# A second layer's attention on one core: values of two units in one product, reciprocals folded into the turn

## The chip, the cores and the metric

One core of one Trainium2 chip. The metric is the device time of one launch in microseconds, the median of the runs shown. Engines: PE is TensorE, DVE VectorE, ACT ScalarE, POOL GpSimd, SP SyncE.

## What is computed

Two transformer layers in fp32 over 256 tokens of width 1024. The change lies in the second one's windowed attention: 16 query heads of 64 columns, 4 key heads, 16 meta tokens that every query sees, and a sink logit for each head. Cut to that:

```python
s_band = jnp.einsum('bqhgd,bkhd->bhgqk', qi, kb).astype(jnp.float32) * scale
s_band = jnp.where(mask, s_band, NEG_INF_2)
s_meta = jnp.einsum('bqhgd,bmhd->bhgqm', qi, k_meta).astype(jnp.float32) * scale
s_sink = jnp.broadcast_to(sink_g[None, :, :, None, None], s_meta.shape[:-1] + (1,))
p = jax.nn.softmax(jnp.concatenate([s_band, s_meta, s_sink], axis=-1), axis=-1)
...
return (jnp.einsum('bhgqk,bkhd->bqhgd', p_band, vb)
        + jnp.einsum('bhgqm,bmhd->bqhgd', p_meta, v_meta))
```

The other half of this layer's attention is differential: 8 heads, two softmaxes each, their difference times the values.

## The kernel before

All weights come as a stream of blobs of 128 x 2048 fp32 (`raw`), which ScalarE copies to a rounded high part (`hi`, L891) and VectorE subtracts to a low part (`lo`, L1901). A product of the weights is then three fp32r products (high by high, high by low, low by high; `product`, L530 to L532, or wider forms at L709 and L711). Every engine has its whole order written out by hand and they meet through semaphores.

In the second layer PE goes through blobs `m2 = 0..33` in two parts each. After each part comes `slot(q)` with `q = 2 * m2 + part`. Small work of the attention is done in the slots, one **unit** a slot, in a pipeline several slots deep. A unit is two heads (`u = 0, 1`) for 128 queries; two neighbouring units `U = 2c, 2c + 1` are the same heads for the first and second 128 queries (`unit_place`). Units 0 to 15 (`U < S_UNITS`) are the windowed attention and units 16 to 31 the differential one; `U0` is 22. Unit U runs so, its slot counted as `q - U0 - U`:

- 0, PE: scores of both heads, four products of 272 columns in fp32r (L1802), to banks 4 and 5.
- 1, DVE: `unit_front` scales, masks and takes the maximum (L2103), into `sc`. ACT: exp of both heads with their sums (L1204) and of the sink (L1207). DVE: `unit_back` adds the sink and takes the reciprocal (L2119, L2120). ACT: `sc` times the reciprocal, one ACTIVATE for each head (L1239), which signals `u_norm`.
- 2, PE: `unit_turn` turns 2 x 2 tiles of 128 x 128 (L1736) and one tile of 48 columns with both heads' meta probabilities (L1739) by `pe.transpose` against `ident`. DVE copies the four tiles to `puT` (L2449), ACT the fifth to `pmT` (L1215).
- 3, PE: `unit_values`: meta (L1750) and two key tiles (L1755) for each head, into 64 columns of the array each, 128 moving columns, plain fp32. ACT and DVE take high and low parts of the result (L1223, L2455).

In one slot of PE, `unit_turn` of a unit stands ahead of `unit_values` of the unit before it, and the scores of a later unit come last. So slot 24 (U0 + 2) has a turn and no values, slots 25 to 39 have both, and slot 40 has values of unit 15 behind the turn of unit 16. A differential unit turns two tiles and a tile of 32 columns; its difference of softmaxes is made before the turn by DVE, and its values are products of full width (L1758, L1760).

`PE` in the text is the group of matmul records, `PEld` that of weight loads. The trace gives one record for a transpose and two for a plain fp32 product.

Of the kernel before, what the change touches and what calls it, by code (L numbers as in the profile page):

```python
# [44 lines left out]
SECOND = TOK + QUAD  # L45
XSTEP = 320


# [139 lines left out]
def build(nc, w, x, meta, consts, turns, rows, grow, out):  # L188

    with ExitStack() as ctx:  # L190
        def sem(name):
            return ctx.enter_context(nc.semaphore(name))
# [119 lines left out]
        rrow2 = at("rrow2", [P, TOK], F32, top[0])  # L312
        ql = [new("ql0", [P, 2, TOK], F32R)]
        assert top[0] <= 3 * BLOB
# [6 lines left out]
        vb_meta = new("vb_meta", [P, D])  # L321
        top[0] += 1536 - 960
        dT_h = at("dT_h", [P, KC, TOK], F32R, top[0])
# [7 lines left out]
        sc = [new("sc0", [P, SECOND + KEYS]), new("sc1", [P, SECOND + KEYS])]  # L331
        puT = new("puT", [P, 4, P])
        pmT = new("pmT", [P, P])
        scratch2 = new("scratch2", [P, 2 * DH])
# [121 lines left out]
        u_pr = sem("u_pr")  # L456
        u_norm = sem("u_norm")
        u_pt = sem("u_pt")
# [424 lines left out]
        def _(act):  # L883
# [300 lines left out]
            for q in range(2 * OUT2):  # L1184
# [9 lines left out]
                if q in VALUES_AT:  # L1194
                    values_out(VALUES_AT[q])
                if q == 14:
                    act.wait_ge(lam_s, 1)
                    act.activation(lam[:, 2:4], lam[:, 0:2], ACT.Exp).then_inc(lam_e, 1)
# [11 lines left out]
                if 0 <= U < UNITS:  # L1210
                    act.wait_ge(u_pt, U + 1)
                    if U:
                        act.wait_ge(u_o, U)
                    rows_used = QUAD + N_META if U < S_UNITS else QUAD
                    act.activation(pmT[0:rows_used, :], ps[0:rows_used, 7, 32:32 + P], ACT.Copy).then_inc(u_ptm, 1)  # L1215
                U = q - U0 - 3
                if 0 <= U < S_UNITS:
                    act.wait_ge(u_o, U + 1)
                    if U == 0:
                        act.wait_ge(kd_out[0], 16 * 5)  # L1220
                        act.wait_ge(kd_out[1], 16 * 2)
                    cc, t = unit_place(U)
                    act.activation(sT_h[:, cc, t * P:(t + 1) * P], ps[:, 7, 288:288 + P],  # L1223
                                   ACT.Copy).then_inc(d_hi, 1)
                elif S_UNITS <= U < UNITS:
                    act.wait_ge(u_o, U + 1)
                    act.wait_ge(u_pr, U + 1)
                    if U >= S_UNITS + 3:

                        act.wait_ge(d_ps, U - S_UNITS - 2)  # L1230
                    first = usoft[:, U % 4, 5, 0:1]
                    act.activation(o_junk[:], ps[:, 7, 288:288 + P], ACT.Square, scale=first,
                                   accum_out=ostat[:, U % 3, 0:1])
                    act.activation(o_tok[U % 3][:], ps[:, 7, 288:288 + P], ACT.Copy, scale=first).then_inc(d_o, 1)
                U = q - U0 - 1
                if 0 <= U < S_UNITS:
                    act.wait_ge(u_pr, U + 1)
                    for u in range(2):
                        ins = act.activation(scores(U, u), scores(U, u), ACT.Copy, scale=usoft[:, U % 4, 5, u:u + 1])  # L1239
                    ins.then_inc(u_norm, 1)  # L1240
                U = q - U0 - 5
# [7 lines left out]
                if q % 2 == 1 and m - 2 in KEY_BLOBS:  # L1249
                    keys_high(m - 2)  # L1250
                if q % 2 == 1 and m - 2 in QUERIES:
                    queries_high(m - 2)
# [176 lines left out]
        def _(pe):  # L1429
# [296 lines left out]
            def unit_turn(U):  # L1726

                pe.wait_ge(u_norm if U < S_UNITS else u_pr, U + 1)
                if U:
                    pe.wait_ge(u_ptd, U)  # L1730
                    pe.wait_ge(u_ptm, U)
                result_read(U - 1)
                heads = 2 if U < S_UNITS else 1
                for u in range(heads):
                    for kt in range(NT):
                        pe.transpose(ps[:, 6, (2 * u + kt) * P:(2 * u + kt + 1) * P],  # L1736
                                     scores_of_tile(U, u, kt), ident)
                both = SECOND + N_META if heads == 2 else SECOND
                pe.transpose(ps[0:both - TOK, 7, 32:32 + P], sc[U % 2][:, TOK:both], ident).then_inc(u_pt, 1)  # L1739

            def unit_values(U):

                pe.wait_ge(u_ptd, U + 1)
                pe.wait_ge(u_ptm, U + 1)
                result_read(U)
                (cc, t), o = unit_place(U), ps[:, 7, 288:288 + P]
                if U < S_UNITS:
                    for u in range(2):
                        a = (2 * (cc // 4) + u) * DH
                        pe.matmul(ps[u * DH:(u + 1) * DH, 7, 288:288 + P], vs_meta[:, a:a + DH], pmT[:],  # L1750
                                  start=True, stop=False)
                    for kt in range(NT):
                        for u in range(2):
                            a = (2 * (cc // 4) + u) * DH
                            m = pe.matmul(ps[u * DH:(u + 1) * DH, 7, 288:288 + P], vs[:, kt, a:a + DH],  # L1755
                                          puT[:, 2 * u + kt, :], start=False, stop=kt == 1)
                else:
                    pe.matmul(o, pmT[:], vb_meta[:, cc * P:(cc + 1) * P], start=True, stop=False)  # L1758
                    for kt in range(NT):
                        m = pe.matmul(o, puT[:, kt, :], vb[:, kt, cc * P:(cc + 1) * P], start=False, stop=kt == 1)  # L1760
                m.then_inc(u_o, 1)

            def slot(q):
# [15 lines left out]
                if 0 <= U + 1 < UNITS:  # L1779
                    unit_turn(U + 1)  # L1780
                if 0 <= U < S_UNITS:
                    unit_values(U)
                U = q - U0 - 5
# [6 lines left out]
                if 0 <= U < UNITS:  # L1790
                    cc, t = unit_place(U)
                    if t == 0:
                        pe.wait_ge(q_in[query_of(U)], 32)
                        pe.wait_ge(kb_in[key_slot(U)], keys_loaded(U))
                    if U:
                        pe.wait_ge(u_max, U)
                    if U > 5:
                        pe.wait_ge(d_lo, U - 5)
                    qT, kT = qs if U < S_UNITS else qd, kB[key_slot(U)]
                    for u in range(2):  # L1800
                        for v in range(2):
                            m = pe.matmul(ps[:, 4 + u, 0:KEYS], qT[u][:, cc, t * P:(t + 1) * P],  # L1802
                                          kT[:, 2 * u + v, 0:KEYS].bitcast(F32R), start=v == 0, stop=v == 1)
                    m.then_inc(u_sc, 1)
# [83 lines left out]
        def _(dve):  # L1888
# [225 lines left out]
            def unit_back(U):  # L2114
# [3 lines left out]
                if U < S_UNITS:  # L2118
                    link(dve, "dve", dve.tensor_tensor(st[:, 4, :], st[:, 4, :], st[:, 3, :], ALU.add))  # L2119
                ins = dve.reciprocal(st[:, 5, :], st[:, 4, :])  # L2120
                if U >= S_UNITS:
                    link(dve, "dve", ins)
                    link(dve, "dve", dve.scalar_tensor_tensor(out=st[:, 3, 0:1], in0=st[:, 5, 1:2], scalar=neglam[:],
                                                              in1=st[:, 4, 0:1], op0=ALU.mult, op1=ALU.mult))
                    first, second = scores(U, 0), scores(U, 1)
                    ins = dve.scalar_tensor_tensor(out=first, in0=second, scalar=st[:, 3, 0:1],
                                                   in1=first, op0=ALU.mult, op1=ALU.add)
                ins.then_inc(u_pr, 1)

# [270 lines left out]
            for q in range(2 * OUT2):  # L2400
# [42 lines left out]
                U = q - U0 - 2  # L2443
                if 0 <= U < UNITS:
                    dve.wait_ge(u_pt, U + 1)
                    if U:
                        dve.wait_ge(u_o, U)
                    n = 4 if U < S_UNITS else 2
                    dve.tensor_copy(puT[:, 0:n, :], ps[:, 6, 0:n * P].rearrange("p (a q) -> p a q", a=n)).then_inc(  # L2449
                        u_ptd, 1)  # L2450
                U = q - U0 - 3
                if 0 <= U < S_UNITS:
                    dve.wait_ge(d_hi, U + 1)
                    cc, t = unit_place(U)
                    dve.tensor_tensor(sT_l[:, cc, t * P:(t + 1) * P], ps[:, 7, 288:288 + P],  # L2455
                                      sT_h[:, cc, t * P:(t + 1) * P], ALU.subtract).then_inc(d_lo, 1)
                if q in (50, 54):
# [296 lines left out]
```

## Time and profile before

| | |
|---|---|
| median of the 3 runs | 869.05 us (868.91 to 869.34) |
| the profiled execution | 870.0 us, of which its span is 868.2 |
| PE busy | 858.9 us, 99% of the span |
| DVE busy | 626.8 us, 72% |
| ACT busy | 478.7 us, 55% |
| windowed units, first turn to last values | 473.3 to 553.0 us (record starts) |

A row of a group reads: line, engine, operation, output <- inputs, shape, xcount, then busy time and the mean of one in ns, then the idle time ahead of it. A matmul's mean is the time of one record from its start to its end, 270 ns and more, and successive ones overlap. What it costs PE is the distance from its start to the next start, which the timeline gives; a line of the timeline merges records of one kind ("x4").

### The profile page before, as it was taken

To read this page: it belongs to the slowest core of one execution; us is meant where nothing else is said; L and a number is where in the kernel's file an instruction comes from. 1 tells how busy PE (TensorE), PEld (TensorE's weight loads), DVE (VectorE), ACT (ScalarE), POOL (GpSimd) and SP (SyncE) were. 2 spreads that over 40 slices of the span, in tenths; PEclk is the share of its full clock that TensorE was granted. 3 is DMA by queue.
4 is the path that set the end of the run, shared out by engine and by line. 5 is a ranking of instruction groups with operands and counts; after the bars stand their busy time and mean duration, and the time that the engine had idled before them with its cause. 6 is when DMAs were issued, how large, how long until landed. Compare 5 with 4: busy or idle time off the path is not lost.

```text
span 868.2 us, 13077 instructions
## 1 busy us (share of the span) xinstructions
PE 858.9 (99%) x4812; PEld 736.2 (85%) x4812; DVE 626.8 (72%) x985; ACT 478.7 (55%) x769; POOL 68.9 (8%) x96
## 2 busy tenths in 40 slices
PE   8999999999999999999999999999999999999997
PEld 6887788888888888889999888888888888888885
DVE  6867677666876666677688887887766876666665
ACT  6546633434644444446687887676653654444443
POOL 1000000000200000002122010132300100000000
PEclk9999999999999999999999999999999999999999
DMA  8955344554565555452766535745475365455531
GB/s 322 415 213 193 110 168 160 183 182 169 186 242 194 193 193 189 143 177 72 249 229 235 173 107 184 259 170 195 152 285 170 122 237 186 172 200 186 178 145 48
DMA packets 30334, 164.70 MB, mean 190 GB/s; under 512 B 3840, under 2 KB 5632, under 8 KB 12880
## 3 DMA queue, kind: packets, MB, share of 16 engines
q1 hardware_dynamic: 27840, 157.71, 51.1%
q10 hardware_dynamic: 2448, 6.37, 2.2%
q8 instruction: 29, 0.48, 0.2%
q14 instruction: 17, 0.14, 0.0%
HBM read 157.02 MB, written 3.83 MB: 185 GB/s over the span
## 4 chain that ended last, share of the span: by engine, by line
PE 97%; DVE 1%; DMA 1%; ACT 0%; issue 0%; SPq 0%; DVEq 0%; POOL 0%; ACTq 0%
PE ps L530 18%; PE ps L532 18%; PE ps L531 18%; PE ps L696 8%; PE ps L681 8%; PE ps L700 4%; PE ps L677 4%; PE ps L709 3%; PE ps L1802 2%; PE ps L711 2%; PE ps L565 1%; PE ps L1736 1%; PE ps L1760 1%; PE ps L1755 1%; PE ps L1750 1%; DMA raw<-weights 1%
## 5 line engine op out<-in xcount | busy, mean ns | idle before, releaser
L1901 DVE TENSOR_TENSOR wlo<-raw,whi 128x2048 fp32r<-128x2048 f32 x134 | 306.9, 2292 | 148.6 <-ACT whi L891 148.0
L891 ACT ACTIVATE whi<-raw 128x2048 fp32r<-128x2048 f32 x134 | 256.3, 1913 | 177.9 <-PE ps L532 108.5
L530 PE MATMUL ps<-whi,xT 128*128 128x512 f32 x192 | 76.8, 400 | 0.0
L532 PE MATMUL ps<-whi,xT 128*128 128x512 f32 x192 | 75.0, 391 | 0.0
L531 PE MATMUL ps<-wlo,xT 128*128 128x512 f32 x192 | 74.9, 390 | 0.0
L1371 POOL TENSOR_TENSOR stat<-stat,cst 128x1 f32<-128x1 f32 x10 | 11.9, 1201 | 489.2 <-DVE stat L1921 260.8
L530 PE MATMUL ps<-whi,fT_h 128*128 128x512 f32 x128 | 50.2, 392 | 0.0
L532 PE MATMUL ps<-whi,fT_l 128*128 128x512 f32 x128 | 49.8, 389 | 0.0
L531 PE MATMUL ps<-wlo,fT_h 128*128 128x512 f32 x128 | 49.8, 389 | 0.0
L530 PE MATMUL ps<-x_all,whi 128*128 128x272 f32 x160 | 46.4, 290 | 0.0
L532 PE MATMUL ps<-x_all,wlo 128*128 128x272 f32 x160 | 46.2, 289 | 0.0
L531 PE MATMUL ps<-x_all,whi 128*128 128x272 f32 x160 | 46.2, 288 | 0.0
L1204 ACT ACTIVATE sc<-sc,usoft 128x272 f32<-128x272 f32 x64 | 32.6, 511 | 19.1 <-DVE usoft L2112 16.0
L532 PEld LDWEIGHTS ps<-whi,xT 128*128 128x128 f32 x192 | 36.0, 188 | 7.8
L530 PEld LDWEIGHTS ps<-whi,xT 128*128 128x128 f32 x192 | 36.1, 188 | 7.4
L531 PEld LDWEIGHTS ps<-wlo,xT 128*128 128x128 f32 x192 | 36.1, 188 | 7.0
L681 PE MATMUL ps<-x_all,whi 128*128 128x512 f32 x176 | 42.0, 391 | 0.0
L530 PE MATMUL ps<-whi,x_all 128*128 128x512 f32 x96 | 38.0, 396 | 0.0
L696 PE MATMUL ps<-x_all,whi 128*128 128x512 f32 x160 | 38.0, 390 | 0.0
L532 PE MATMUL ps<-whi,x_all 128*128 128x512 f32 x96 | 37.8, 393 | 0.0
L681 PEld LDWEIGHTS ps<-x_all,whi 128*128 128x128 f32 x176 | 32.3, 188 | 6.3
L531 PE MATMUL ps<-wlo,x_all 128*128 128x512 f32 x96 | 37.5, 391 | 0.0
(351 smaller groups left out, 1885.3 us busy)
## 6 DMA issues: line engine op xcount, KB each, us to landing
raw<-weights SPq DMA_DIRECT2D x134, 1024.0 KB, 4.8
kB<-key_parts SPq DMA_DIRECT2D x20, 272.0 KB, 3.3
key_parts<-knat SPq DMA_DIRECT2D x4, 544.0 KB, 3.0
cst<-consts SPq DMA_DIRECT2D x1, 1371.0 KB, 13.4
kswap<-kraw SPq DMA_DIRECT2D x8, 136.0 KB, 2.4
raw<-weights SPq DMA_DIRECT2D x4, 256.0 KB, 6.1
raw<-weights SPq DMA_DIRECT2D x2, 512.0 KB, 7.5
gate_a<-gain_rows ACTq DMA_DIRECT2D x2, 512.0 KB, 8.1
```

The costliest lines, as they stand in the source:

```text
L530: pe.matmul(o, lh, rh, start=first, stop=False)
L531: pe.matmul(o, lh, rl, start=False, stop=False)
L532: return pe.matmul(o, ll, rh, start=False, stop=last)
L677: pe.matmul(ps[:, bank0 + j, 0:TOK], vl[:, k, j * P:(j + 1) * P], x[:, 0, k, :], start=k == 0, stop=False, skip_group_check=True)
L681: m = pe.matmul(ps[:, bank0 + j, :], vh[:, k, j * P:(j + 1) * P], x[:, :, k, :], start=False, stop=k == KC - 1, skip_group_check=True)
L696: pe.matmul(ps[:, bank0 + j, :], vh[:, k, j * P:(j + 1) * P], x[:, :, k, :], start=k == 0, stop=False)
L700: m = pe.matmul(ps[:, bank0 + j, 0:TOK], vl[:, k, j * P:(j + 1) * P], x[:, 0, k, :], start=False, stop=k == KC - 1)
L709: pe.matmul(ps[:, bank + j, :], vh[:, k, j * P:(j + 1) * P], x2[:, :, k, :], start=k == 0, stop=False)
L711: m = pe.matmul(ps[:, bank + j, 0:TOK], vl[:, k, j * P:(j + 1) * P], x2[:, 0, k, :], start=False, stop=k == KC - 1)
L891: act.activation(whi[s][:], raw[s][:], ACT.Copy).then_inc(split_hi, 1)
L1204: ins = act.activation(scores(U, u), scores(U, u), ACT.Exp, bias=st[:, 2, u:u + 1], accum_out=st[:, 4, u:u + 1])
L1901: dve.tensor_tensor(wlo[s][:], raw[s][:], whi[s][:], ALU.subtract).then_inc(split_lo, 1)
```

## The change

For the windowed units alone:

- The ACTIVATEs that multiply by the reciprocals are gone. VectorE makes two diagonal matrices `unit_diag` (`ident` times the reciprocal, one for each head) in `unit_back`, and the turn is a plain fp32 product of the probabilities with that diagonal instead of a transpose. The tile with the meta probabilities becomes two products, of 32 and 16 columns, as each head has its own diagonal.
- The copy of the four turned tiles goes from VectorE to ScalarE. `puT` and `pmT` are doubled, with one half for each unit of a pair.
- The values are made once for a pair of units (`pair_values`), with 256 moving columns instead of 128, in every second slot. The high and low parts are taken once a pair.
- `queries_high` of blobs 9 and 12 goes one slot later, behind `values_out`. PE's scores wait for fewer semaphores. `ql0`, `puT` and what lies around them have other addresses.

```diff
@@ ScalarE
                 if q in VALUES_AT:
                     values_out(VALUES_AT[q])
+                    if m - 3 in QUERIES:
+                        queries_high(m - 3)
...
                     act.wait_ge(u_pt, U + 1)
-                    if U:
-                        act.wait_ge(u_o, U)
+                    if U > 1:
+                        act.wait_ge(u_o, U - U % 2 if U < S_UNITS else U - 1)
...
-                    act.activation(pmT[0:rows_used, :], ps[0:rows_used, 7, 32:32 + P], ACT.Copy).then_inc(u_ptm, 1)
-                U = q - U0 - 3
-                if 0 <= U < S_UNITS:
-                    act.wait_ge(u_o, U + 1)
+                    if U < S_UNITS:
+                        act.activation(puT[:, :, U % 2, :], ps[:, 6, :].rearrange("p (a q) -> p a q", a=4),
+                                       ACT.Copy).then_inc(u_ptd, 1)
+                    act.activation(pmT[0:rows_used, U % 2, :], ps[0:rows_used, 7, 32:32 + P], ACT.Copy).then_inc(u_ptm, 1)
+                U = q - U0 - 4
+                if 0 <= U < S_UNITS and U % 2 == 0:
+                    act.wait_ge(u_o, U + 2)
...
+                    act.activation(sT_h[:, cc, :], ps[:, 7, PAIR:PAIR + TOK], ACT.Copy).then_inc(d_hi, 2)
...
-                U = q - U0 - 1
-                if 0 <= U < S_UNITS:
-                    act.wait_ge(u_pr, U + 1)
-                    for u in range(2):
-                        ins = act.activation(scores(U, u), scores(U, u), ACT.Copy, scale=usoft[:, U % 4, 5, u:u + 1])
-                    ins.then_inc(u_norm, 1)
@@ TensorE
             def unit_turn(U):
...
+                for u in range(2):
+                    for kt in range(NT):
+                        pe.matmul(ps[:, 6, (2 * u + kt) * P:(2 * u + kt + 1) * P], scores_of_tile(U, u, kt),
+                                  unit_diag[:, U % 2, u, :], start=True, stop=True)
+                for u, (a, b) in enumerate(((TOK, SECOND), (SECOND, SECOND + N_META))):
+                    m = pe.matmul(ps[a - TOK:b - TOK, 7, 32:32 + P], sc[U % 2][:, a:b], unit_diag[:, U % 2, u, :],
+                                  start=True, stop=True)
+                m.then_inc(u_pt, 1)
+
+            def pair_values(U):
+
+                pe.wait_ge(u_ptd, U + 2)
+                pe.wait_ge(u_ptm, U + 2)
+                result_read(U)
+                cc, _ = unit_place(U)
+                for u in range(2):
+                    a = (2 * (cc // 4) + u) * DH
+                    pe.matmul(ps[u * DH:(u + 1) * DH, 7, PAIR:PAIR + TOK], vs_meta[:, a:a + DH],
+                              pmT[:].rearrange("p a q -> p (a q)"), start=True, stop=False)
+                for kt in range(NT):
+                    for u in range(2):
+                        a = (2 * (cc // 4) + u) * DH
+                        m = pe.matmul(ps[u * DH:(u + 1) * DH, 7, PAIR:PAIR + TOK], vs[:, kt, a:a + DH],
+                                      puT[:, 2 * u + kt].rearrange("p a q -> p (a q)"), start=False, stop=kt == 1)
+                m.then_inc(u_o, 2)
...
-                if 0 <= U < S_UNITS:
-                    unit_values(U)
+                if 1 <= U < S_UNITS and U % 2 == 1:
+                    pair_values(U - 1)
@@ VectorE
                 if U < S_UNITS:
                     link(dve, "dve", dve.tensor_tensor(st[:, 4, :], st[:, 4, :], st[:, 3, :], ALU.add))
+                    link(dve, "dve", dve.reciprocal(st[:, 5, :], st[:, 4, :]))
+                    if U >= 2:
+                        dve.wait_ge(u_pt, U - 1)
+                    for u in range(2):
+                        ins = dve.tensor_scalar(unit_diag[:, U % 2, u, :], c("ident"), st[:, 5, u:u + 1], None, ALU.mult)
+                    ins.then_inc(u_diag, 1)
```

How the order moves is seen at two places. The first is PE, two successive slots with the turns of units 3 and 4 (`sc` is the probabilities, `x_all` the tokens' products between the slots, left out here). Before, both slots read alike but for the buffer; the first one:

```order
L1736 MATMUL ps<-cst,sc_143 128x128 [waits u_ptm,d_lo,u_ptd,u_norm]
L1736 MATMUL ps<-cst,sc_143 128x128 x3
L1739 MATMUL ps<-cst,sc_143 48x128
L1750 MATMUL ps<-pmT,vs_meta 64x128 [waits d_lo,u_ptm,u_ptd]
L1750 MATMUL ps<-pmT,vs_meta 64x128
L1755 MATMUL ps<-puT,vs 64x128 x4
L1802 MATMUL ps<-kB_121,qs_133 128x272 [waits u_max]
```

The same slot in the change, and (behind the "...", and behind its own four rows of the turn) the values in the slot after it:

```order
L1742 MATMUL ps<-unit_diag,sc_144 128x128 [waits u_ptm,d_lo,u_ptd,u_diag]
L1742 MATMUL ps<-unit_diag,sc_144 128x128 x3
L1745 MATMUL ps<-unit_diag,sc_144 32x128
L1745 MATMUL ps<-unit_diag,sc_144 16x128
L1816 MATMUL ps<-kB_121,qs_134 128x272 [waits u_max]
...
L1757 MATMUL ps<-pmT,vs_meta 64x256 [waits d_lo,u_ptm,u_ptd]
L1757 MATMUL ps<-pmT,vs_meta 64x256
L1762 MATMUL ps<-puT,vs 64x256 x4
```

The values left the first slot and stand in the second with twice the columns; the turn has one instruction more in both. The second place is ScalarE, from one unit's exps to the next unit's. Before:

```order
L1204 ACTIVATE sc_143,usoft<-sc_143,usoft 128x272
L1207 ACTIVATE usoft<-usoft 128x2
L1215 ACTIVATE pmT<-ps 48x128 [waits u_o,u_pt]
L1223 ACTIVATE sT_h<-ps 128x128 [waits u_o]
L1239 ACTIVATE sc_143<-sc_143,usoft 128x272 [waits u_pr]
```

In the change, the slot with a pair's result in it:

```order
L1209 ACTIVATE sc_144,usoft<-sc_144,usoft 128x272
L1212 ACTIVATE usoft<-usoft 128x2
L1221 ACTIVATE puT<-ps 128x4x128 [waits u_o,u_pt]
L1223 ACTIVATE pmT<-ps 48x128
L1231 ACTIVATE sT_h<-ps 128x256 [waits u_o]
```

The two ACTIVATEs of L1239 (one for each head; one row is shown) are gone, and one copy of 512 columns stands ahead of `pmT`.

## Rows read from the trace of the kernel before

**Rows 1.** The page: busy shares, granted clock, and the chain that ended last.

```profile
span 868.2 us, 13077 instructions
PE 858.9 (99%) x4812; PEld 736.2 (85%) x4812; DVE 626.8 (72%) x985; ACT 478.7 (55%) x769; POOL 68.9 (8%) x96
...
PEclk9999999999999999999999999999999999999999
...
PE 97%; DVE 1%; DMA 1%; ACT 0%; issue 0%; SPq 0%; DVEq 0%; POOL 0%; ACTq 0%
```
**Rows 2.** Waits by line, 460 to 640 us: who waited <- for whom: us, times, longest.

```profile
ACT pmT L1215 <- PE ps L1755: 10.3, 13, 1.8
...
PEld ps L1750 <- issue: 3.3, 16, 0.2
...
PEld ps L1773 <- ACT kraw L1165: 0.3, 1, 0.3
```
**Rows 3.** Timeline, PE, two slots of the stage: start us, us, line, shapes, xcount.

```profile
507.44 0.60 PE L1736 MATMUL ps<-cst,sc 128*128 128x128 f32 x4
507.88 0.27 PE L1739 MATMUL ps<-cst,sc 128*48 128x128 f32 x1
508.08 0.44 PE L1750 MATMUL ps<-pmT,vs_meta 128*64 128x128 f32 x4
508.35 0.61 PE L1755 MATMUL ps<-puT,vs 128*64 128x128 f32 x8
508.88 0.77 PE L1802 MATMUL ps<-kB,qs 128*128 128x272 f32 x4
509.50 0.29 PE L530 MATMUL ps<-x_all,whi 128*128 128x272 f32 x1
...
512.51 0.60 PE L1736 MATMUL ps<-cst,sc 128*128 128x128 f32 x4
```
**Rows 4.** Timeline, PE, the first unit: a turn with no values behind it.

```profile
473.26 0.60 PE L1736 MATMUL ps<-cst,sc 128*128 128x128 f32 x4
...
473.72 0.75 PE L1802 MATMUL ps<-kB,qs 128*128 128x272 f32 x4
```
**Rows 5.** Timeline, PE, a unit of the second half.

```profile
591.38 0.39 PE L1758 MATMUL ps<-vb_meta,pmT 128*128 128x128 f32 x2
591.60 0.61 PE L1760 MATMUL ps<-vb,puT 128*128 128x128 f32 x4
592.04 0.38 PE L1736 MATMUL ps<-cst,sc 128*128 128x128 f32 x2
```
**Rows 6.** Timeline, PE, first block: plain fp32 products with 256 moving columns.

```profile
135.54 0.59 PE L1638 MATMUL ps<-vr,decayed 128*128 128x256 f32 x2
135.97 0.60 PE L1639 MATMUL ps<-vr,decayed 128*128 128x256 f32 x2
```
**Rows 7.** Groups of PE by line and shape, whole span: us busy, mean ns of one.

```profile
L1736 PE MATMUL ps<-cst,sc 128*128 128x128 f32 x96 | 15.7, 272 | 0.0
...
L1760 PE MATMUL ps<-vb,puT 128*128 128x128 f32 x64 | 9.8, 275 | 0.0
```
**Rows 8.** Groups of ScalarE, 470 to 560 us.

```profile
L1239 ACT ACTIVATE sc<-sc,usoft 128x272 f32<-128x272 f32 x32 | 14.9, 515 | 3.5 <-DVE usoft L2120 3.4
...
L1139 ACT ACTIVATE kraw<-ps 128x512 f32<-128x512 f32 x4 | 2.3, 576 | 0.0
```
**Rows 9.** Groups of VectorE, 470 to 560 us.

```profile
L2449 DVE COPY puT<-ps 128x512 f32<-128x512 f32 x16 | 11.0, 687 | 0.8 <-PE ps L1755 0.8
...
L2455 DVE TENSOR_TENSOR sT_l<-ps,sT_h 128x128 fp32r<-128x128 f32 x16 | 4.5, 280 | 0.0
```
**Rows 10.** Timelines of ScalarE, then VectorE, in the slot that begins at 507.44 us.

```profile
509.53 0.25 ACT L1215 ACTIVATE pmT<-ps 48x128 f32<-48x128 f32 x1
...
510.19 0.94 ACT L1239 ACTIVATE sc<-sc,usoft 128x272 f32<-128x272 f32 x2 [0.25 <-DVE usoft L2120]
...
510.07 0.69 DVE L2449 COPY puT<-ps 128x512 f32<-128x512 f32 x1
```

More of the change, by code:

```diff
@@ L46 @@
 XSTEP = 320
+PAIR = 160
 MIX1 = 2 + 1 + 2 + 2 + 4 + 4 + 4 + 4 + 2 + 4 + 4
@@ L312, in build @@
         rrow2 = at("rrow2", [P, TOK], F32, top[0])
-        ql = [new("ql0", [P, 2, TOK], F32R)]
+        top[0] += 2 * P
+        puT = new("puT", [P, 4, NT, P])
         assert top[0] <= 3 * BLOB
@@ L321, in build @@
         vb_meta = new("vb_meta", [P, D])
-        top[0] += 1536 - 960
+        ql = [new("ql0", [P, 2, TOK], F32R)]
+        top[0] += 1024 - 960
         dT_h = at("dT_h", [P, KC, TOK], F32R, top[0])
@@ L331, in build @@
         sc = [new("sc0", [P, SECOND + KEYS]), new("sc1", [P, SECOND + KEYS])]
-        puT = new("puT", [P, 4, P])
-        pmT = new("pmT", [P, P])
+        pmT = new("pmT", [P, NT, P])
+        unit_diag = new("unit_diag", [P, 2, 2, P])
         scratch2 = new("scratch2", [P, 2 * DH])
@@ L456, in build @@
         u_pr = sem("u_pr")
-        u_norm = sem("u_norm")
+        u_diag = sem("u_diag")
         u_pt = sem("u_pt")
@@ L1221, in _ @@
                         act.wait_ge(kd_out[1], 16 * 2)
[L1222 to L1225, printed above, removed]
+                    cc, _ = unit_place(U)
+                    act.activation(sT_h[:, cc, :], ps[:, 7, PAIR:PAIR + TOK], ACT.Copy).then_inc(d_hi, 2)
+                U = q - U0 - 3
+                if S_UNITS <= U < UNITS:
                     act.wait_ge(u_o, U + 1)
-                    act.wait_ge(u_pr, U + 1)
+                    act.wait_ge(u_pr, U - S_UNITS + 1)
                     if U >= S_UNITS + 3:
@@ L1234, in _ @@
                     act.activation(o_tok[U % 3][:], ps[:, 7, 288:288 + P], ACT.Copy, scale=first).then_inc(d_o, 1)
-                U = q - U0 - 1
-                if 0 <= U < S_UNITS:
-                    act.wait_ge(u_pr, U + 1)
-                    for u in range(2):
-                        ins = act.activation(scores(U, u), scores(U, u), ACT.Copy, scale=usoft[:, U % 4, 5, u:u + 1])
-                    ins.then_inc(u_norm, 1)
                 U = q - U0 - 5
@@ L1250, in _ @@
                     keys_high(m - 2)
-                if q % 2 == 1 and m - 2 in QUERIES:
+                if q % 2 == 1 and m - 2 in QUERIES and q + 1 not in VALUES_AT:
                     queries_high(m - 2)
@@ L1726, in unit_turn @@
             def unit_turn(U):
-                pe.wait_ge(u_norm if U < S_UNITS else u_pr, U + 1)
+                pe.wait_ge(u_diag if U < S_UNITS else u_pr, U % S_UNITS + 1)
                 if U:
@@ L1731, in unit_turn @@
                     pe.wait_ge(u_ptm, U)
-                result_read(U - 1)
-                heads = 2 if U < S_UNITS else 1
-                for u in range(heads):
+                result_read((U - 1) // 2 * 2 if U <= S_UNITS else U - 1)
+                if U >= S_UNITS:
                     for kt in range(NT):
[L1736 to L1739, printed above, removed]
+                        pe.transpose(ps[:, 6, kt * P:(kt + 1) * P], scores_of_tile(U, 0, kt), ident)
+                    pe.transpose(ps[0:QUAD, 7, 32:32 + P], sc[U % 2][:, TOK:SECOND], ident).then_inc(u_pt, 1)
+                    return
+                for u in range(2):
[10 more added lines that the diff above has]
+                result_read(U)
+                cc, _ = unit_place(U)
+                for u in range(2):
[8 more added lines that the diff above has]
+                m.then_inc(u_o, 2)
             def unit_values(U):
@@ L1746, in unit_values @@
                 (cc, t), o = unit_place(U), ps[:, 7, 288:288 + P]
[L1747 to L1760, printed above, removed]
+                pe.matmul(o, pmT[:, t, :], vb_meta[:, cc * P:(cc + 1) * P], start=True, stop=False)
+                for kt in range(NT):
+                    m = pe.matmul(o, puT[:, kt, t, :], vb[:, kt, cc * P:(cc + 1) * P], start=False, stop=kt == 1)
                 m.then_inc(u_o, 1)
@@ L1796, in slot @@
                         pe.wait_ge(u_max, U)
-                    if U > 5:
+                    if U - 5 > S_UNITS:
                         pe.wait_ge(d_lo, U - 5)
@@ L2119, in unit_back @@
                     link(dve, "dve", dve.tensor_tensor(st[:, 4, :], st[:, 4, :], st[:, 3, :], ALU.add))
-                ins = dve.reciprocal(st[:, 5, :], st[:, 4, :])
-                if U >= S_UNITS:
-                    link(dve, "dve", ins)
+                    link(dve, "dve", dve.reciprocal(st[:, 5, :], st[:, 4, :]))
[4 more added lines that the diff above has]
+                    ins.then_inc(u_diag, 1)
+                else:
+                    link(dve, "dve", dve.reciprocal(st[:, 5, :], st[:, 4, :]))
                     link(dve, "dve", dve.scalar_tensor_tensor(out=st[:, 3, 0:1], in0=st[:, 5, 1:2], scalar=neglam[:],
@@ L2125, in unit_back @@
                     first, second = scores(U, 0), scores(U, 1)
-                    ins = dve.scalar_tensor_tensor(out=first, in0=second, scalar=st[:, 3, 0:1],
-                                                   in1=first, op0=ALU.mult, op1=ALU.add)
-                ins.then_inc(u_pr, 1)
+                    dve.scalar_tensor_tensor(out=first, in0=second, scalar=st[:, 3, 0:1],
+                                             in1=first, op0=ALU.mult, op1=ALU.add).then_inc(u_pr, 1)
             dve.memset(kaT[:], 0.0).then_inc(init_ok, 1)
@@ L2443, in _ @@
                 U = q - U0 - 2
-                if 0 <= U < UNITS:
+                if S_UNITS <= U < UNITS:
                     dve.wait_ge(u_pt, U + 1)
[L2446 to L2449, printed above, removed]
+                    dve.wait_ge(u_o, U - 1)
+                    dve.tensor_copy(puT[:, 0:2, U % 2, :], ps[:, 6, 0:TOK].rearrange("p (a q) -> p a q", a=2)).then_inc(
                         u_ptd, 1)
[L2451 to L2456, printed above, removed]
+                U = q - U0 - 4
+                if 0 <= U < S_UNITS and U % 2 == 0:
+                    dve.wait_ge(d_hi, U + 2)
+                    cc, _ = unit_place(U)
+                    dve.tensor_tensor(sT_l[:, cc, :], ps[:, 7, PAIR:PAIR + TOK], sT_h[:, cc, :],
+                                      ALU.subtract).then_inc(d_lo, 2)
                 if q in (50, 54):
```

## The prediction

> **What bounds the kernel now.** I read the page first: PE is busy for 858.9 of 868.2 us, the chain that ended last is PE for 97% of the span, and the granted clock is in its top tenth in all 40 slices, the 2.4 GHz level [rows 1]. VectorE at 72% and ScalarE at 55% have room on the average, so the question for the stage is whether PE ever waits for them there. The waits say no. From 460 to 640 us ScalarE waits for PE (10.3 us at the pmT copy), while the weight loads show one wait of 0.3 us for kraw and 16 gaps of 0.2 us at L1750 that no engine released [rows 2]. So the time is the sum of what PE issues, and I price PE's slots by the distance from start to start in the timeline. Work taken off ScalarE or VectorE is worth nothing here unless PE work goes with it.
>
> **Prices on PE.** Four transposes and one more take 0.44 us up to the start of the fifth, 0.109 us each [rows 3]. L1736 has 96 records for 16 x 4 + 16 x 2 = 96 transposes, one each, whereas L1760 has 64 for 32 plain products, two each [rows 7]. Those records are 0.11 us apart too: 0.22 us for two, 0.44 us for four [rows 5]. So a plain fp32 product with 128 moving columns costs two transposes, 0.218 us. With 256 columns a record takes 0.43 / 2 = 0.215 to 0.218 us [rows 6]: the cost goes by columns, with nothing fixed to save. Products of 64 output columns come at 0.27 us for four records and 0.53 us for eight [rows 3], about 0.055 to 0.067 us each, so the two heads' columns work side by side: two records in one step of 0.109 us. Around them lies what the change of array shape costs. From L1739 to L1750 there are 0.20 us where 0.11 is the pitch (+0.09), the four L1750 records take 0.27 where two steps make 0.22 (+0.05), and the eight L1755 records last 0.53 up to the scores where four steps make 0.44 (+0.09), in all 0.23 us for each block of values [rows 3]. Without values behind it, the turn is followed at once: 0.46 us from its start to the scores [rows 4].
>
> **The slots, before.** With turn and values 508.88 - 507.44 = 1.44 us [rows 3]. There are 15 of them (25 to 39), and slot 24 with 0.46 [rows 4]: 22.06 us. In slot 40 the values add 0.09 + 0.27 + 0.53 = 0.89 us.
>
> **The slots, after.** The four tiles' turn is eight records, 0.87 us instead of 0.44: 16 x 0.436 = **+7.0 us**, the largest term and one with direct rows. The meta tile turns by two products of 32 and 16 columns in different parts of the array. The trace of before has no such product. I take L1750, the nearest, also two narrow products on two parts: 0.09 to enter, 0.27, 0.09 to leave, 0.45 us, where the one transpose took 0.11. A slot with only a turn is then 0.87 + 0.45 = 1.32 us. With a pair's values there come a second change of shape (32 to 64 columns, 0.09), two steps of 0.218 for the meta keys with the same 0.05, four steps of 0.218, and the leaving that is counted already: 0.87 + 0.09 + 0.27 + 0.09 + 0.49 + 0.87 + 0.09 = 2.77 us. Turn-only slots are 24, 25, 27 to 39 odd, nine; slots with both are 26 to 38 even, seven: 9 x 1.32 + 7 x 2.77 = 31.27 us. In slot 40 the values take 0.09 + 0.49 + 0.87 + 0.09 = 1.54 us, 0.65 more than before. Sum: 31.27 - 22.06 + 0.65 = **+9.9 us**. The values themselves give nothing back: 16 x 6 steps of 0.109 = 10.5 us become 8 x 6 steps of 0.218 = 10.5 us. Nor do the changes of shape become fewer, as the narrow meta products now make one in each slot.
>
> **Bounds.** Lower, the meta products might change no shape and cost just two steps (0.22): slots of 1.09 and 2.63 us, +6.8 us. Upper, their four records might run one after another, 0.22 us more in each of 16 units: +13.4 us. Between them I stay with L1750, as it is the one row with two narrow products.
>
> The Trainium skill would move two of these terms. "TensorE: Matmul & The Clock Gate", section Terms, calls the transpose mode 4x faster for FP32; the rows make it 2x, and what a factor of four would give stands as a rival below. "TensorEngine Tiling (Array Packing)", section Instruction Overhead, gives each matmul some 60 cycles of overhead and so speaks for wider moving operands. By that page (an estimate of 25 ns in each of the 8 x 6 steps that go) pairing would return 1.2 us and the sum be +8.7; the rows at 128 and 256 columns show no such fixed part, so I leave it out.
>
> **The other engines.** In a slot ScalarE loses two ACTIVATEs of 0.515 us and gains a copy of 512 columns, about 0.58 as L1139 [rows 8]; the result's high part comes half as often. VectorE loses 0.69, and half of the 0.28 passes, for two diagonals of at most 0.28 each by the nearest row of that width [rows 9]. Both get lighter while PE gets longer. The waits: the turn needed the scaled probabilities, ready at 510.19 + 0.94 = 511.13 us for a turn at 512.51, 1.4 us early [rows 3, 10]. Now it needs the diagonals; the reciprocal was over by 510.07, so they are there by 510.7, 1.8 us early. It also needs both copies of the turn before; starting where pmT did, at 509.53, they end by 510.4 [rows 10]. Queued behind ScalarE's wait for u_o are pmT and the pair's high part, then VectorE's low part, which the turn after next waits for; these come a slot earlier than needed and the cover is the 3.0 us of products between the slots [rows 3]. If it failed, the next late thing would be that low part. The later queries_high stands in the same order ahead of POOL and SP's stores for units four slots off or more: nothing. It may remove the 0.3 us wait for kraw [rows 2]; I leave that out. DMA traffic is the same. After the stage PE has no wait that could take the loss back.
>
> Against the profiled execution: span 868.2 + 9.9 = 878.1, its own time 870.0 + 9.9 = 879.9. The median of the runs is 0.95 lower than that execution, so 869.05 + 9.9 = **878.9 us**.
>
> **Rivals.**
> - The narrow meta products in series, without side-by-side work: +13.4, 882.5 us. For it: no row has 32 or 16 plain columns. Against: L1750. 0.13.
> - PE comes to wait for the copies that now stand on ScalarE, behind the exps. From about 1.8 us of delay it decides; if each pair lost 0.6 us, +4.8 more, 883.7 us. For it: one engine now makes both copies and the high part. Against: ScalarE's own waits for PE [rows 2]. 0.05.
> - A plain fp32 product costs four transposes, 0.436 us. Then 16 x 4 x 0.327 = +20.9 us stand for the first term instead of 7.0, and with the rest 893 us. Against: two records at the same pitch [rows 5, 7]. 0.02. (This is the factor of four of the Trainium skill's "TensorE: Matmul & The Clock Gate", Terms.)
> - Faster: a product with a diagonal takes one pass like a transpose, one record at 0.109 us, and the narrow pair one step without a change of shape. Then the turn costs what it did (+0.1 in slot 24) and pairing saves eight blocks' changes of shape, 8 x 0.23 = 1.84 us: 867.3 us. It decides as soon as a turn product shows one record. Nothing in [rows 5, 7] speaks for it, as L1760 also multiplies a plain fp32 operand by another. 0.03.
> - No change: PE's added work lands in waits of PE that the trace hides. Its start-to-start distances leave none above the pitch [rows 3 to 5]. 0.02.
>
> **How the numbers follow.** The forecast has 0.75. The range runs from the lower bound, 869.05 + 6.8 = 875.9, with 0.4 for rounding, to the serial rival's 882.5: 875.5 to 882.6, which leaves out the stalls, the factor of four and the two cases without loss, and the tails of the forecast. A measurement of this kernel tells some 0.2% (1.7 us) from no change; slower by more than that are the forecast and the first three rivals, 0.95; the same 0.02; faster 0.03.
>
> **What would show it.** In the profile after: the turn's product with 128 records (16 x 4 x 2), the first meta record about 0.96 us behind the turn's first; turn-only slots near 1.32 us and full ones near 2.77 us; six steps of 0.218 us in pair_values; no waits of PE on u_diag, u_ptd or d_lo; ScalarE some 0.4 us a slot lighter. I am wrong if the turn products come as single records, if a 256-column step of 64-wide products is well under 0.2 us, or if PE shows waits.

## The result and the profile after

879.01 us median against 869.19 before (six runs of each); the ratio of the runs is 1.0107 (95% interval 1.0096 to 1.0118), so the change costs 9.3 us (8.3 to 10.3), where the two medians are 9.8 apart. One of the six runs of the change took 1756.5 us and is left out of the ratio; without it the median is 879.00. The profiled execution took 879.03 us with a span of 877.2, against 870.0 and 868.2.

The page, span and busy shares, which answer to [rows 1]:

```profile
span 877.2 us, 13082 instructions
...
PE 867.9 (99%) x4828; PEld 741.0 (84%) x4828; DVE 628.7 (72%) x993; ACT 472.5 (54%) x745; POOL 68.9 (8%) x96
```

PE is busy for 9.0 us more and the span is 9.0 us longer. ScalarE lost 6.2 us of work (478.7 to 472.5) and VectorE gained 1.9, and the span shows neither. PE's timeline in two slots of the stage (start us, us, line, shapes, xcount), the answer to [rows 3]: the first with a turn and a pair's values, the second with a turn only.

```profile
504.96 1.06 PE L1742 MATMUL ps<-unit_diag,sc 128*128 128x128 f32 x8
505.95 0.41 PE L1745 MATMUL ps<-unit_diag,sc 128*32 128x128 f32 x4
506.28 0.65 PE L1757 MATMUL ps<-pmT,vs_meta 128*64 128x256 f32 x4
506.77 1.03 PE L1762 MATMUL ps<-puT,vs 128*64 128x256 f32 x8
507.73 0.77 PE L1816 MATMUL ps<-kB,qs 128*128 128x272 f32 x4
...
511.13 1.05 PE L1742 MATMUL ps<-unit_diag,sc 128*128 128x128 f32 x8
512.11 0.41 PE L1745 MATMUL ps<-unit_diag,sc 128*32 128x128 f32 x4
512.45 0.77 PE L1816 MATMUL ps<-kB,qs 128*128 128x272 f32 x4
```

From the turn to the scores the full slot takes 507.73 - 504.96 = 2.77 us and the other 1.32 us. The four tiles and the way into the narrow products (those on 16, 32 or 64 of the array's columns) take 0.99, the meta tile 0.33 to 0.34 with the way out, the pair's meta products 0.49, its key tiles 0.96 with the way out. The groups of PE (us busy, mean ns of one) give the counts that [rows 7] answer to:

```profile
L1742 PE MATMUL ps<-unit_diag,sc 128*128 128x128 f32 x128 | 16.8, 274 | 0.0
...
L1762 PE MATMUL ps<-puT,vs 128*64 128x256 f32 x64 | 8.3, 379 | 0.0
...
L1745 PE MATMUL ps<-unit_diag,sc 128*32 128x128 f32 x32 | 6.5, 285 | 0.0
L1745 PE MATMUL ps<-unit_diag,sc 128*16 128x128 f32 x32 | 6.3, 278 | 0.0
...
L1757 PE MATMUL ps<-pmT,vs_meta 128*64 128x256 f32 x32 | 5.2, 404 | 0.0
```

L1742 has 128 records for 64 products, two each. The waits from 460 to 640 us (who <- for whom: us, times, longest): what PE's weight loads show from 0.2 us a time at the changed lines, the longest of ScalarE at the moved work, and the one wait of the weight loads for an engine.

```profile
PEld ps L1816 <- issue: 4.9, 17, 0.4
...
PEld ps L1757 <- issue: 1.6, 8, 0.2
...
ACT puT L1221 <- PE ps L1762: 17.1, 7, 3.5
...
PEld ps L1772 <- DVE puT L2465: 0.2, 1, 0.2
```

The gaps of 0.2 us and more that no engine released stand where the width of the products changes (128*128, 128*64, 128*32 in the rows; "change of shape" from here on), now 17 at the scores and 8 at the pair's meta products; two more of 0.2 us at the differential units' transposes were there before. Before, they were the 16 of [rows 2] and, in the same view, another 16 at the scores:

```profile
PEld ps L1802 <- issue: 2.7, 16, 0.2
```

The one wait for an engine is 0.2 us at the first differential values, behind the paired units. The 0.3 us wait for kraw of [rows 2] is gone. ScalarE waits for PE before its new copy, and PE not for it.

### The profile page after: what moved, and what is told of

It is laid out like the page before. It is cut to its first block, busy times and chain, and to the rows that moved or that the text cites. A ratio compares the mean times of both kernels' runs of the same rounds, so it can differ in the third digit from the quotient of the medians.

```text
span 877.2 us, 13082 instructions
## 1 busy us (share of the span) xinstructions
PE 867.9 (99%) x4828; PEld 741.0 (84%) x4828; DVE 628.7 (72%) x993; ACT 472.5 (54%) x745; POOL 68.9 (8%) x96
## 4 chain that ended last, share of the span: by engine, by line
PE 98%; DMA 1%; DVE 1%; ACT 0%; SPq 0%; DVEq 0%; issue 0%; POOL 0%; ACTq 0%
PE ps L533 18%; PE ps L535 18%; PE ps L534 18%; PE ps L699 8%; PE ps L684 7%; PE ps L703 4%; PE ps L680 4%; PE ps L712 3%; PE ps L1816 2%; PE ps L714 2%; PE ps L1742 2%; PE ps L568 1%; PE ps L1774 1%; PE ps L1762 1%; DMA raw<-weights 1%; PE ps L1745 1%
```

## The experiments

Every kernel was timed beside the kernel before on its chip (869.5 us there for the diagonals alone, the meta tile, the copy and pairing alone, 869.6 for the other four); differences to the change are taken between the distances to it, +9.8 us for the change itself.

**Diagonals alone.** Values are made for each unit again, 128 moving columns in each slot, and ScalarE's wait for them goes by the unit:

```diff
-                if 1 <= U < S_UNITS and U % 2 == 1:
-                    pair_values(U - 1)
+                if 0 <= U < S_UNITS:
+                    one_values(U)
```

> The change with the values made per unit again (128 moving columns, each slot), all else as changed. Theory: slots of 1.32 + 0.27 + 0.53 = 2.12 us, 15 of them, 1.32 in slot 24 and 0.89 for the values of slot 40, in all 34.0 us against 32.8 in the change: +1.2 us, 880.2 us. All of the loss then comes from the turn. Rival (pairing is part of the loss): at or under 879.0 us.

Measured: 880.3 us (ratio to before 1.0118, 1.0103 to 1.0134). PE's timeline, one slot:

```profile
511.90 1.05 PE L1742 MATMUL ps<-unit_diag,sc 128*128 128x128 f32 x8
...
513.48 0.61 PE L1762 MATMUL ps<-puT,vs 128*64 128x128 f32 x8
514.02 0.77 PE L1833 MATMUL ps<-kB,qs 128*128 128x272 f32 x4
```

2.12 us as forecast (2.12 to 2.13 in all fifteen slots). It is +10.8 us, 1.0 more than the change where 1.2 was expected. The intervals of the two ratios overlap, so the slot's length in the trace carries this more than the times do (a pair takes 2 x 2.12 = 4.24 us here and 1.32 + 2.77 = 4.09 in the change): pairing was a small gain inside the change, and all of the loss lies in the turn.

**The meta tile turned by one transpose**, its columns multiplied beforehand on VectorE:

```diff
-                for u, (a, b) in enumerate(((TOK, SECOND), (SECOND, SECOND + N_META))):
-                    m = pe.matmul(ps[a - TOK:b - TOK, 7, 32:32 + P], sc[U % 2][:, a:b], unit_diag[:, U % 2, u, :],
-                                  start=True, stop=True)
-                m.then_inc(u_pt, 1)
+                both = SECOND + N_META
+                pe.transpose(ps[0:both - TOK, 7, 32:32 + P], sc[U % 2][:, TOK:both], ident).then_inc(u_pt, 1)
...
+                    for u in range(2):
+                        a = SECOND if u else TOK
+                        dve.tensor_scalar(sc[U % 2][:, a:a + N_META], sc[U % 2][:, a:a + N_META], st[:, 5, u:u + 1], None, ALU.mult)
```

> The change, but the tile of meta probabilities is turned by one transpose of 48 columns again; VectorE multiplies its two times 16 columns by the reciprocals beforehand. Theory (the narrow products cost two steps and a change of shape of the array): slots of 0.91 instead of 1.32 us and 2.53 instead of 2.77: -5.4 us, 873.6 us. Rival (narrow products cost only their two steps, the shape costs nothing): 16 x 0.11 = -1.7 us, 877.3 us.

Measured: 873.45 us (ratio 1.0044, 1.0029 to 1.0059). PE's timeline, a slot of each kind:

```profile
508.65 1.05 PE L1742 MATMUL ps<-unit_diag,sc 128*128 128x128 f32 x8
509.54 0.27 PE L1745 MATMUL ps<-cst,sc 128*48 128x128 f32 x1
509.56 0.75 PE L1814 MATMUL ps<-kB,qs 128*128 128x272 f32 x4
...
513.16 1.05 PE L1742 MATMUL ps<-unit_diag,sc 128*128 128x128 f32 x8
...
515.70 0.52 PE L1814 MATMUL ps<-kB,qs 128*128 128x272 f32 x2
```

0.91 us (509.56 - 508.65) and 2.54 us (515.70 - 513.16), where 0.91 and 2.53 were expected. It is +3.9 us, 5.9 less than the change (5.3 by the lengths of the slots). Two products of 48 columns together cost over half of the whole loss, and of this only 16 x 0.11 = 1.7 us are their columns. The rival with free changes of shape is out. That the shape is the cause of the rest is read from where the gaps stand; no run changed the shape alone.

**Each turn product twice**, to price one by the end-to-end time:

```diff
-                    for kt in range(NT):
+                    for kt in (0, 0, 1, 1):
                         pe.matmul(ps[:, 6, (2 * u + kt) * P:(2 * u + kt + 1) * P], scores_of_tile(U, u, kt),
                                   unit_diag[:, U % 2, u, :], start=True, stop=True)
```

> The change with each of the four plain turn products of a unit made twice, 64 more in all, into the same place. Theory (a plain fp32 product of 128 columns costs two records of 0.109 us on PE): +14.0 us, 893.0 us. Rival (part of PE's time at the turn is waiting that more products would fill): less than +12 us; rival (four passes of 0.109 us): +27.9 us.

Measured: 893.22 us, +23.6 (two runs, ratio 1.0273, 1.0253 to 1.0292). The group, and one turn in PE's timeline:

```profile
L1742 PE MATMUL ps<-unit_diag,sc 128*128 128x128 f32 x256 | 31.1, 275 | 0.0
...
510.15 1.95 PE L1742 MATMUL ps<-unit_diag,sc 128*128 128x128 f32 x16
512.03 0.41 PE L1745 MATMUL ps<-unit_diag,sc 128*32 128x128 f32 x4
```

256 records; 13.8 us more than the change for 64 products, 0.215 us each (the two profiled spans, 891.3 and 877.2, give 0.220), and sixteen records with the way into the narrow products in 512.03 - 510.15 = 1.88 us. Two records of 0.11 us each it is, and PE had no slack at the turn that they could have filled.

**The copy of the turned tiles back on VectorE**, the rest as changed:

```diff
-                        act.activation(puT[:, :, U % 2, :], ps[:, 6, :].rearrange("p (a q) -> p a q", a=4),
-                                       ACT.Copy).then_inc(u_ptd, 1)
...
+                    dve.tensor_copy(puT[:, :, U % 2, :], ps[:, 6, :].rearrange("p (a q) -> p a q", a=4)).then_inc(u_ptd, 1)
```

> The change with the copy of the turned tiles back on VectorE. Theory (neither engine is waited for): no difference, 879.0 within 0.5 us. Rival (the copy on ScalarE makes PE wait): faster by 1 to 5 us.

Measured: 879.21 us, +9.7, as the change. In the change the place of the copy costs nothing and gives nothing.

**Pairing alone.** Transposes, ScalarE's two ACTIVATEs and VectorE's copy as in the kernel before; values once a pair:

```diff
-                        pe.matmul(ps[:, 6, (2 * u + kt) * P:(2 * u + kt + 1) * P], scores_of_tile(U, u, kt),
-                                  unit_diag[:, U % 2, u, :], start=True, stop=True)
+                        pe.transpose(ps[:, 6, (2 * u + kt) * P:(2 * u + kt + 1) * P], scores_of_tile(U, u, kt), ident)
...
+                    act.wait_ge(u_diag, U + 1)
+                    for u in range(2):
+                        ins = act.activation(scores(U, u), scores(U, u), ACT.Copy, scale=usoft[:, U % 4, 5, u:u + 1])
+                    ins.then_inc(u_norm, 1)
```

(`u_diag` is signalled by the reciprocal here.)

> The change without the diagonals and without the move of the copy: transposes, ScalarE multiplies by the reciprocals, VectorE copies puT, values once a pair. Theory (the time is the sum of PE's start-to-start distances): the turn is back to 0.46 us where nothing follows it, a slot with a pair's values is 0.54 + 0.09 + 0.49 + 0.96 = 2.08 us. 9 x 0.46 + 7 x 2.08 against 22.13 us before, and +0.65 in slot 40: -2.7 us, about -0.3 more with the later queries_high. 866.2 us, 0.3% faster than before. Rival (pairing gives nothing or costs: later copies and a doubled step of 64-wide products): 869 us or more.

Measured: 868.7 us, ratio 0.9986 (0.9977 to 0.9995): faster than before, but by 1.2 us (0.4 to 2.0) and not by 3. The slots have their forecast lengths, and PE waits instead. PE's timeline in two slots, and the waits of PE and its weight loads from 460 to 650 us:

```profile
540.64 0.60 PE L1746 MATMUL ps<-cst,sc 128*128 128x128 f32 x4
...
542.72 0.77 PE L1817 MATMUL ps<-kB,qd 128*128 128x272 f32 x4
...
546.08 0.60 PE L1746 MATMUL ps<-cst,sc 128*128 128x128 f32 x4
...
546.54 0.75 PE L1817 MATMUL ps<-kB,qd 128*128 128x272 f32 x4
...
PEld ps L1741 <- DVE sc L2141: 1.3, 1, 1.3
...
PEld ps L1788 <- ACT kraw L1169: 0.4, 1, 0.4
PE ps L713 <- ACT vb L1185: 0.2, 1, 0.2
```

2.08 and 0.46 us. So the sum of the slots was right: from the first turn to the scores behind the turn of unit 16, the 17 slots take 20.7 us here and 23.3 before. But the stretches between them grew from 56.6 to 58.7 us, because the condition under which the sum is the time (nobody is waited for) had gone, as PE now came sooner to each turn. The largest wait is at the turn of unit 16, the first whose probabilities VectorE must combine. VectorE's and PE's timelines there, and ScalarE's at the wait for kraw:

```profile
548.34 0.16 DVE L2137 RECIPROCAL usoft<-usoft 128x2 f32<-128x2 f32 x1
548.54 1.16 DVE L2138 SCALAR_TENSOR_TENSOR usoft<-usoft,neglam 128x1 f32<-128x1 f32 x1
549.74 0.50 DVE L2141 SCALAR_TENSOR_TENSOR sc<-sc,usoft 128x272 f32<-128x272 f32 x1
550.16 0.68 DVE L2462 COPY puT<-ps 128x512 f32<-128x512 f32 x1
...
550.94 0.41 PE L1741 MATMUL ps<-cst,sc 128*128 128x128 f32 x2 [0.91 <-DVE sc L2141]
...
499.68 0.94 ACT L1245 ACTIVATE sc<-sc,usoft 128x272 f32<-128x272 f32 x2 [1.37 <-DVE usoft L2135]
500.52 0.60 ACT L1169 ACTIVATE kraw<-ps 128x544 f32<-128x544 f32 x1
```

The profile puts PE's wait down to the difference L2141. That was over at 550.24, while PE starts at 550.94, 0.1 us behind the end of the copy of unit 15's tiles (550.16 + 0.68), for which the turn also waits. So here too the copy ended last, behind the low part of the weights and the difference. ScalarE stands 1.37 us in its wait for the reciprocal, with the copy of kraw queued behind its two ACTIVATEs, and PE's L1788 waits for that copy.

**The unit's difference first.** As pairing alone, but unit 16's `unit_back` ahead of the low part of the weights (2.29 us) in slot 39:

```diff
+                if U == S_UNITS:
+                    unit_back(U)
                 if q % 2 == 1 and 1 <= m2:
                     lo(N1 + m2 + 2)
...
-                if 0 <= U < UNITS:
+                if 0 <= U < UNITS and U != S_UNITS:
                     unit_back(U)
```

> The kernel with paired values alone (e1), and VectorE makes unit 16's difference ahead of that slot's weight low part instead of behind it. Theory: e1 lost 1.0 us of its 2.7 in the one wait of PE for VectorE at the turn of unit 16; it goes: 867.7 to 867.9 us, 0.8 to 1.0 under e1. Rival (the wait moves to the low part or to another slot): as e1, 868.7 us.

Measured: 868.66 us, ratio 0.9989 (0.9980 to 0.9999); the rival was right. VectorE's timeline, then PE's at the same turn:

```profile
546.77 0.50 DVE L2141 SCALAR_TENSOR_TENSOR sc<-sc,usoft 128x272 f32<-128x272 f32 x1
547.19 2.28 DVE L1916 TENSOR_TENSOR wlo<-raw,whi 128x2048 fp32r<-128x2048 f32 x1
549.39 0.68 DVE L2464 COPY puT<-ps 128x512 f32<-128x512 f32 x1
...
550.18 0.41 PE L1741 MATMUL ps<-cst,sc 128*128 128x128 f32 x2 [0.98 <-issue]
```

The difference is ready at 547.3, and PE still starts at 550.18 after 0.98 us of idle time, 0.1 us behind the end of the copy of unit 15's tiles (549.39 + 0.68), for which the turn also waits. Two things stood behind the same low part, and the later of them, the copy, stayed there.

**More on ScalarE.** Pairing alone, with the copy on ScalarE besides its two ACTIVATEs:

> e1 with the copy of the turned tiles on ScalarE as well, so that ScalarE has the two ACTIVATEs of 0.51 us and the copy of 0.60 us in each slot. Theory (e1's small waits are ScalarE being late): more and longer waits of PE for ScalarE, 870 to 873 us. Rival (ScalarE has room, as its busy share of 54% says): 868.7 us like e1, or 867.8 if VectorE's relief removes the wait at unit 16.

Measured: 869.43 us, ratio 0.9999 (0.9990 to 1.0009): pairing's gain is gone, about 1 us by the two ratios, whose intervals just overlap. The wait at unit 16 is gone, as VectorE is relieved, and the waits for ScalarE have grown, so that the stretches between the slots take 59.4 us against 58.7 (waits of PE and its loads, 460 to 650 us):

```profile
PEld ps L1791 <- ACT kraw L1169: 1.3, 2, 0.8
...
PE ps L534 <- ACT vb L1185: 0.6, 2, 0.3
PEld ps L1749 <- ACT sc L1248: 0.5, 1, 0.5
```

The direction was right and the size too large (the theory had 1.3 us more at the least); VectorE's relief, which I had only in the rival, took one wait off in return. ScalarE, busy for 56% of the span, is late in this stage.

**Both relieved.** Paired values, transposes, no ACTIVATE for the reciprocals: VectorE multiplies in place, ScalarE copies the tiles, unit 16's difference first:

```diff
+                    link(dve, "dve", dve.reciprocal(st[:, 5, :], st[:, 4, :]))
+                    for u in range(2):
+                        ins = dve.tensor_scalar(scores(U, u), scores(U, u), st[:, 5, u:u + 1], None, ALU.mult)
+                    ins.then_inc(u_norm, 1)
```

> Paired values and transposes; the product with the reciprocals is made in place by VectorE (two TENSOR_SCALAR of 272 columns) and ScalarE copies the turned tiles; unit 16's difference first. Theory: e1's small waits of PE (0.9 us in three places) come from ScalarE, which held the value copies behind the two ACTIVATEs; without these all of the sum comes through: -2.7 us to the kernel before and the kraw wait too, 866.2 to 866.6 us. Rival (VectorE, now with 2 x 0.4 us for 0.69, is late and PE waits for it): 868 us or more.

Measured: 866.54 us, ratio 0.9965 (0.9953 to 0.9978), within the forecast. This version beats both kernels, the one before by 3.0 us (1.9 to 4.1). The waits of PE's weight loads, 460 to 650 us, all of them:

```profile
PEld ps L1814 <- issue: 3.1, 8, 0.4
PEld ps L1755 <- issue: 1.6, 8, 0.2
PEld ps L1800 <- issue: 0.4, 2, 0.2
```

Only gaps that no engine released are left. The slots take 20.6 us and the stretches between them 56.3, against 23.3 and 56.6 before, so the whole of -2.7 us for pairing and -0.3 for kraw came through once nobody was late. Three things were moved at once here, so the run does not say which of them each wait needed.

## Why the prediction was right

The forecast was +9.9 us and 878.9; +9.8 by the medians, +9.3 (8.3 to 10.3) by the ratio, and 879.01 came out. That the time fell within 0.1 us is luck, as the interval is ten times as wide; the terms are what can be judged. By its steps:

- **What bounds.** PE waited for no engine at the windowed units, and 6.2 us less work on ScalarE did nothing. The copy moved back to VectorE changed nothing, and 64 more products cost their full 13.8 us. So in the change PE issues without a break, and the sum of its distances is the time.
- **Two records for a plain product.** 128 records at L1742, a price of 0.215 us by the doubled turn against the 0.218 used. The term of 7.0 us stands. The rival at four times a transpose's cost would have given +27.9 for the doubled turn; in these traces the transpose is 2x as fast. The Trainium skill's "TensorE: Matmul & The Clock Gate", section Terms, calls the transpose mode 4x faster for FP32; the measurement decides against it.
- **The meta tile.** L1750 was the right neighbour: 0.33 us with the way out, and 0.12 for the way in, 0.45 in all. Turning it by a transpose took 5.9 us off, 5.4 expected. The way in was 0.03 us longer than the 0.09 of L1750 and the rest 0.03 shorter, so that the slots came out to the hundredth is in part two small errors that cancel. The serial rival, 0.22 us more in each unit, is out.
- **The values.** 0.49 + 0.96 us for a pair, the steps of 0.218 us. Nothing came back from wider operands, as argued: a step is 0.109 us at 128 columns and 0.218 at 256. The Trainium skill's "TensorEngine Tiling (Array Packing)", section Instruction Overhead, gives each matmul some 60 cycles of overhead; no such part shows at these widths.
- **The sum.** The slots came at 1.32 and 2.77 us, both to the hundredth. From the first scores to the end the execution takes 877.2 - 473.99 = 403.2 us where it took 868.2 - 473.72 = 394.5 [rows 4]: 8.7 more, and 0.86 for the first turn ahead of them make 9.6. Nearly all of the 0.3 us to 9.9 stands in the stretches between the slots, which take 56.35 us against 56.60. Of this 0.17 is one place: before, PE began the transposes of kraw at 501.87 us, right behind ScalarE's copy of it (501.22 + 0.60), a second wait for kraw, too short for the 0.2 us of the list; in the change that stretch takes 4.06 us instead of 4.23. PE reached the first turn 0.6 us sooner after the start of its span, so the profiled executions differ by 9.0 only. About half of it is the wait for kraw at 472.5 us, which I had left out of the sum; the other 0.3 us was there at the scores before it. The first scores after:

```profile
473.99 0.77 PE L1816 MATMUL ps<-kB,qs 128*128 128x272 f32 x4
```

- **The wrong part** lay in the reading of the other engines, and it did no harm where PE got slower. The prediction gave slacks of 1.4 and 1.8 us from one slot and let them stand for all sixteen. Pairing alone takes 2.7 us from PE over the whole stage, and it met waits at several slots, up to 0.9 us of PE: one at the turn, where the last thing was a copy behind the low part, and the others at ScalarE's copies of kraw and vb, which the prediction had not priced. The slack of a stage is that of its tightest slot. It also had VectorE get lighter, and it got 1.9 us heavier: the copies and low parts against the diagonals gave 4.4 us back as priced (11.0 + 4.5 before, 7.7 + 3.4 after), and two lines of small instructions took 4.2 more (L2122 and L2124, 9.4 us against 5.2), for the reason in the last section. And of the gaps without a releaser it names only those at L1750; the 16 at the scores are in its start-to-start distances all the same, so the sum lost nothing by it.

## What to carry to other kernels

On an engine that never waits, price an edit by the start-to-start distances and the number of records that it makes, and look for prices at the nearest shapes; another engine's busy share says nothing on what relief is worth. A transpose turned into a plain fp32 product, to save a multiplication on an engine that nobody waits for, doubles that step, and a short block of narrow products costs as much for the change of shape around it (0.23 us) as for its columns (0.22 us here). The same edit can hold a gain: taken apart, the pairing is worth 2.7 us (3.0 with the earlier kraw), if each engine's work is then put where its tightest slot has room.

## What I had not expected of the hardware

VectorE's smallest instructions can take eight times as long. L2122 multiplies 128 x 2 elements and takes a minimum, in 0.16 us in 13 of its 16 executions in the change and in 1.0 to 1.3 us in three; here are VectorE's and GpSimd's timelines of the change at one of the three:

```profile
514.60 1.27 DVE L2122 SCALAR_TENSOR_TENSOR usoft<-usoft,negsink 128x2 f32<-128x2 f32 x1
515.90 0.16 DVE L2124 TENSOR_TENSOR usoft<-usoft,negsink 128x2 f32<-128x2 f32 x1
...
514.55 1.29 POOL L1413 TENSOR_TENSOR ql<-kswap,qd 128x512 fp32r<-128x512 f32 x1 [9.60 <-ACT qd L1158]
```

It starts 0.05 us behind a TENSOR_TENSOR of GpSimd and ends with it, 1.27 us later. All three long ones (470.95, 514.60 and 537.46 us) overlap such an instruction of GpSimd and none of the other 13 does; in the kernel before, the same line never overlaps one and takes 0.16 us all 16 times. In pairing alone the same befell L2138 at 548.54 (1.16 us), in the chain that PE then waited for. Both have two tensor operands in SBUF. The Trainium skill's "SBUF — State Buffer", section Who interferes with whom, says that such an instruction contends with a GpSimd instruction that reads SBUF; the trace agrees in these rows. Two such operands are not the whole condition: the TENSOR_SCALAR of L2126, with one, starts at 559.19 us in the change and takes 1.04 us instead of 0.17, up to the end of GpSimd's next one (558.90 + 1.30). No run took GpSimd's work away to show it alone. In a chain of small instructions between two engines this is 1 us that no other row hints at.
